# Gather groups 2 and 3 of a quad moved between the halves of its first gate product

## What is computed

```python
# h: (256, 1024) normed tokens; 16 experts in 4 groups, the best 2 of one group are chosen per token
logits = h @ router_w + router_b
topi, topw = the two best experts of the best group, weights normed to sum 1
# every expert e, on the tokens that chose it:
y_e = (silu(x_e @ w_gate[e]) * (x_e @ w_up[e])) @ w_down[e]      # 1024x512, 1024x512, 512x1024
x = x + sum over the two chosen experts of topw * y_e
```

## Time and profile before

| | |
|---|---|
| median of 3 runs | 1118.53 us (1118.07 to 1119.0) |
| the profiled execution | 1118.4 us |
| its span, first to last instruction | 1116.6 us |
| PE busy | 1092.6 us (98%) |
| DVE busy | 572.4 us (51%) |
| ACT busy | 465.6 us (42%) |
| DMA, mean over the span | 280 GB/s |
| mean granted clock of TensorE | 0.999 |

### The profile page before, as it was taken

How to read it: one execution, slowest core, us unless ns; L and a number is a source line. 1 busy time by engine, 2 the same in 40 slices (tenths; PEclk the granted TensorE clock), 3 DMA queues, 4 the chain that set the end, 5 groups by cost and what they waited for, 6 DMA issues and landing times.

```text
span 1116.6 us, 14331 instructions
## 1 busy us (share of the span) xinstructions
PE 1092.6 (98%) x5822; PEld 755.3 (68%) x5822; DVE 572.4 (51%) x906; ACT 465.6 (42%) x746; POOL 0.2 (0%) x4
## 2 busy tenths in 40 slices
PE   8999999999999999999999999999999999999997
PEld 6998888888886344434379988888888753444432
DVE  6669574656565123323277686745575642323222
ACT  5677565566543001010166856755655420010000
POOL 0000000000000000000000000000000000000000
PEclk9999999999999999999999999999999999999999
DMA  9545454263777999999964344452449699999995
GB/s 373 225 151 187 148 191 154 76 226 151 285 294 311 430 427 428 427 427 428 420 258 181 128 183 151 151 191 92 171 154 368 247 370 430 427 427 428 427 427 247
DMA packets 23955, 313.14 MB, mean 280 GB/s; under 512 B 3153, under 2 KB 3281, under 8 KB 5457
## 3 DMA queue, kind: packets, MB, share of 16 engines
q1 hardware_dynamic: 23616, 312.22, 69.8%
q10 hardware_dynamic: 272, 0.00, 0.0%
HBM read 311.16 MB, written 1.05 MB: 280 GB/s over the span
## 4 chain that ended last, share of the span: by engine, by line
PE 87%; DMA 6%; DVE 4%; ACT 2%; issue 1%; DVEq 0%; SPq 0%
PE slot L639 35%; PE M L971 16%; PE slot L1004 9%; PE slot L622 8%; DMA arena<-in_w_up 6%; PE slot L865 3%; PE slot L930 2%; PE slot L568 2%; PE M L823 1%; PE slot L943 1%; PE M L801 1%; PE M L943 1%; PE M L772 1%; PE M L812 1%; PE M L746 1%
## 5 line engine op out<-in xcount | busy, mean ns | idle before, releaser
L1402 DVE TENSOR_TENSOR w_lo<-ring,w_hi 128x1024 fp32r<-128x1024 f32 x199 | 239.4, 1223 | 153.6 <-ACT w_hi L1061 152.1
L1061 ACT ACTIVATE w_hi<-ring 128x1024 fp32r<-128x1024 f32 x200 | 208.2, 1055 | 102.2 <-PE slot L639 70.6
L639 PE MATMUL slot<-w_hi,hT_hi 128*128 128x512 f32 x480 | 192.5, 401 | 0.0
L639 PE MATMUL slot<-w_lo,hT_hi 128*128 128x512 f32 x480 | 187.3, 390 | 0.0
L639 PE MATMUL slot<-w_hi,hT_lo 128*128 128x512 f32 x480 | 187.0, 390 | 0.0
L1835 DVE TENSOR_TENSOR arena<-arena,M 128x512 f32<-128x512 f32 x16 | 11.0, 688 | 203.4 <-PE M L971 203.4
L639 PEld LDWEIGHTS slot<-w_lo,hT_hi 128*128 128x128 f32 x480 | 90.1, 188 | 19.4
L639 PEld LDWEIGHTS slot<-w_hi,hT_hi 128*128 128x128 f32 x480 | 90.2, 188 | 18.8 <-issue 0.8
L639 PEld LDWEIGHTS slot<-w_hi,hT_lo 128*128 128x128 f32 x480 | 90.3, 188 | 18.1 <-issue 0.5
L622 PE MATMUL slot<-hT_hi,w_hi 128*128 128x256 f32 x256 | 73.4, 287 | 0.0
L622 PE MATMUL slot<-hT_hi,w_lo 128*128 128x256 f32 x256 | 72.4, 283 | 0.0
(11 more groups left out here) (278 smaller groups left out, 1650.2 us busy)
## 6 DMA issues: line engine op xcount, KB each, us to landing
ring<-in_w_mix SPq DMA_DIRECT2D x48, 2048.0 KB, 8.2
ring<-in_w_down SPq DMA_DIRECT2D x18, 2048.0 KB, 19.7
arena<-in_w_gate SPq DMA_DIRECT2D x12, 2048.0 KB, 18.8
ring_down<-in_w_gate SPq DMA_DIRECT2D x12, 2048.0 KB, 20.3
ring<-in_w_up SPq DMA_DIRECT2D x10, 2048.0 KB, 19.8
ring_up<-in_w_up SPq DMA_DIRECT2D x6, 2048.0 KB, 16.8
ring_odd<-in_w_up SPq DMA_DIRECT2D x6, 2048.0 KB, 21.0
arena<-in_w_up SPq DMA_DIRECT2D x6, 2048.0 KB, 22.4
```

The source lines that it names most:

```text
L639: last = mm(o[:, t * 512:(t + 1) * 512], h[:, 2 * n + cc, t * P:(t + 1) * P], w[:, cc * 512:(cc + 1) * 512], start=n == cc == k == 0, stop ...
L1061: A(piece_of(w_hi, i), source(i), ACT.Copy).then_inc(hi_ready.sem, 1)
L1402: v.tensor_tensor(piece_of(w_lo, i), source(i), piece_of(w_hi, i), ALU.subtract)\
```

## The change

Groups 0 and 1 of a quad's gather stay where they are. Groups 2 and 3 are issued inside the even pair of the quad, behind half 0 of stage 0 and before half 1 (ahead of that half's waits). This holds for all quads: the first, the next two, and the one in the loop. The waits' text, DVE, ACT and SP are unchanged.

```diff
                 pe.wait_ge(sel_hot, start // 2 + 1 + l)
-                for r in range(4):
+                for r in range(2):
                     gather(start // 2, r, first=True)
...
                             idx = 2 * stage + h
+                            if idx == 1 and not odd:
+                                for r in range(2, 4):
+                                    gather(it // 2, r, first=first)
                             wv = weights(6 * odd + idx, None if late else 6 * n + idx, it0, late)
...
                         pe.wait_ge(sel_hot, (start + n) // 2 + 1 + l)
-                        for r in range(4):
+                        for r in range(2):
                             gather((start + n) // 2, r)
...
                     pe.wait_ge(sel_hot, it // 2 + 1 + l)
-                    for r in range(4):
+                    for r in range(2):
                         gather(it // 2, r)
```

## The result

| | before | after |
|---|---|---|
| median of 4 runs | 1118.37 us | 1130.22 us (1130.08 to 1130.58) |
| the profiled execution | 1118.4 us | 1130.2 us |
| span | 1116.6 us | 1128.4 us |
| mean granted clock of TensorE | 0.999 | 1.000 |

The ratio is 1.0106, with a 95% interval of 1.0094 to 1.0118: the changed kernel is slower by 11.85 us, 1.1%. Forecast were 1130.7 us.

A forecast was written before the change was run, and what follows sets the result against it. PE and DMA were taken as nearly level in the expert part, with PE 98% busy. PE losses of 7.43 and 7.50 us less 2.6 us of DMA waits gave 1118.4 + 12.3 = 1130.7 us, range 1127.5 to 1133.5.

The forecast's parts named there:

- The two waits: Gate product's first half waits uncovered for group 1's evacuation, its second for group 3's: 1.06 us each, every quad.
- Resuming behind an evacuation: PE was to resume 0.05 us after an evacuation ends, at both waits of a quad.
- Starting on an empty array: Each gate half that starts behind a wait was to cost 0.05 us extra, with bounds 0 and 0.1.
- The switch itself: PE's change from a product to a gather, ahead of groups 2 and 3: 0.13 us.
- The sum a quad: From group 1's last matmul to the second half: 7.67 us against 5.87, +1.80; first quads +2.03 and +2.10.
- What DMA gives back: PE's waits for weights at layer ends vanish, 1.24 and 1.35 us; second landing at 370.5 instead of 369.9.
- The pairs' number for ACT: Its cast moves to about 360.2 us, ahead of ACT's first SiLU with nearly 2 us of cover: no cost.
- The net: PE's losses of 7.43 and 7.50 us in the two layers, less 2.6 us of DMA waits: 12.3 us slower.
- Rival (a): Interposed half product hides the new waits and the bank wait goes: 1118.5 us; 3%, shared with DMA slack covering PE's loss.
- Rival (b): First slot's release 1.2 us earlier pulls each layer's train of weight landings forward: 1116.1 us; 2%.
- (c): Only one of a quad's two evacuation waits is felt: 1123.7 us; 4%.
- (d): PE's clock falls at some new stalls, one half product a quad at 1.2 GHz: 1158 us; 3%.

The follow-up runs named there:

- e1: Changed kernel with groups 0 to 2 ahead of the gate product's first half and only group 3 between the halves: 1125.01 us.
- e2: Changed kernel with groups 2 and 3 moved into the middle of the gate product's first half: 1123.12 us.
- e6: Changed kernel, but the gate product's second half rereads feature blocks 0 to 3, its wait for all evacuations moved ahead of the up product: 1123.24 us.
- the light kernels: Kernel before and changed kernel, each with the last of every pair's six weight transfers cut to an eighth of its columns: 1115.53 and 1130.16 us.
- e4: Kernel before with the last of every pair's six weight transfers cut to an eighth of its columns: 1115.53 us.
- e7: Kernel before with groups 0 to 2 ahead of the gate product and group 3 in the middle of its first half: 1118.99 us.
- e8: Kernel before; in each layer's first pair, group 3 follows gate's first half, then up's first half, both second halves; two transfers swapped: 1118.65 us.
- e9: Changed kernel with PE's pair counter in layer 1 a constant, so its written-out quads there wait against constants: 1130.75 us.

## Why the prediction was right

- **The two waits.** 1.06 us each was forecast for every quad, 1.06 to 1.07 was found in five and 1.15 to 1.22 in three. All 16 waits are there. e1, e2 and e6 show that both cost, and e6 that it is the dependence.
- **Resuming behind an evacuation.** The 0.05 us came from the wait for the bank. It holds (0.05 or 0.06) at the ten waits against a register; at the six against a constant it is 0.15 (in the second quad 411.43 - 410.59 - 0.69). The first of these, 1.22 us, also has its evacuation start 0.06 us later.
- **Starting on an empty array**, 0.05 us twice: no run shows this cost. The half with its switch takes 408.38 - 404.80 = 3.58 us behind the wait, against 3.56 in the earlier trace rows, but in e1, where its wait is covered, it takes 3.58 too (407.63 - 404.05). The switch itself (0.13) and the two groups (1.89) came as forecast.
- **The sum a quad.** Forecast 1.80; found 1.07 + 3.58 + 1.89 + 1.06 - 5.87 = 1.73 in the loop and in layer 1, and 1.16 + 3.58 + 1.89 + 1.16 - 5.87 = 1.92 in the second and third quad of layer 0. The first quads were forecast at 2.03 and 2.10 and lost 2.15 and 1.97 (358.70 - 348.98 = 9.72 against 353.42 + 3.43 - 349.28 = 7.57; 916.72 - 907.22 = 9.50 against 7.53). A layer was forecast at 7.43 and 7.50 us; the light kernels give 7.58 and 7.06. That the whole sum is only 0.3 us off is in part luck: a start-up cost that is not there and a longer resumption in three quads cancel in part.
- **What DMA gives back.** Forecast 1.24 and 1.35 us; e4 measures 1.24 and 1.34. The second landing was put at 370.5 us, and is at 370.25; from the first mark it moved by 0.64 us, where 0.6 was forecast.
- **The pairs' number for ACT.** The cast moved to 359.87 and the first SiLU came at 362.39, when its product was done; nothing was added.
- **The net** was 12.3 us; the two expert parts show 12.16, the medians 11.85. The 0.3 us between these lie ahead of the first mark.
- **Rival (a)**, interposed matmuls as cover. The Trainium skill's rule (Perfetto Trace Analysis, Optimizing Tensor Performance, Matmuls) speaks of independent groups. e7 keeps to it, with group 2 over group 1's evacuation and half a half over group 3's, and shows no such wait; the changed kernel's halves depend on the evacuations that they were to cover. So the trace agrees with the rule as it is worded. The changed order did not give the 1118.5 us that (a) made of it; e7's order, with 1118.99, comes near it.
- **Rival (b)**, the landings pulled forward, gave no gain even where both its conditions held, in e8. Its premise, that the second landing follows the first by one transfer's time (4.9 us), held in neither layer (5.8 and 5.4 us); what layer 1 gained all the same, some 0.4 us at the second landing and 0.15 in the layer, does not stand out of the scatter of the runs. **(c)** is out by e1 and e2, and for **(d)** the clock stayed at 1.00.

In the experiments' expectations the sizes of e1 and e2 were 1.6 and 1.5 us too high. e1 was put at 1.35 us a quad, because of the longer waits of the changed kernel's layer 0, which are those of three quads of eight; its trace has 1.28 us in those three and 1.20 in the other five, so 9.8 - 2.6 = 7.2 us. e2 was put at 8.8 us in all, its trace has 7.7, so 5.1. The two layers of the traces sum to +7.10 and +5.09 us. The remaining 0.4 to 0.5 us, down to the medians, lie for the most part ahead of the first mark, which these executions reached at 348.78 and 349.00 and not at 349.28.

## What to carry to other kernels

Work put between two dependent halves covers a wait only if the half behind it does not need that work's result: list, for every wait that stays, which matmuls now stand between producer and consumer. Putting a part of the producer one step earlier, and the last part inside a half instead of at its end, kept both evacuations covered, for 0.3 us a quad on PE, which the waits for DMA hid here. Where two resources are nearly level, measure the slack of one against the other (here 1.3 us a layer), since it comes off every loss once and hides small ones whole.

## What was not expected of the hardware

- A wait of PE against a constant let the half start 0.1 us later than the same wait against a register: 1.15 to 1.22 us from the last gather matmul at the six waits with a constant in the changed kernel, 1.06 or 1.07 at the ten with a register, and again where e9 swapped the form. The wait for the bank in the kernel before (0.33 or 0.34 us in either form) does not show it.
- In e8 a 2 MB transfer issued 4.7 us behind another, with nothing else queued at that time, landed 5.8 us behind it in layer 0 and 5.4 in layer 1, where the full queue has 4.9 us a transfer (2 MB at 427 GB/s).
